# One of two input row buffers begins 48 bytes later in its rows, and the split weights that meet it move with it

## The reference

```python
def hybrid_layer(x, ...):
    h = rms_norm(x, norm1_w)
    (rq, rk, rv, rg, dq, dk, dv, cb, cc, cx, gates) = [h @ w_in[:, s:e] for s, e in column_bounds()]
    ...
    merged = (g[:, :, 0] * (ret @ w_branch[0]) + g[:, :, 1] * (diff @ w_branch[1])
              + g[:, :, 2] * (conv @ w_branch[2]))
    x = x + merged @ w_out
    u = jnp.square(jax.nn.relu(rms_norm(x, norm2_w) @ w_up))
    return x + u @ w_down

def second_block(x, ...):
    proj = hn_p @ w_in[l]
    ...
    mix = (gate_sb * (sb @ w_sb_out[l]) + gate_gla * (o @ w_gla_out[l])) @ w_o[l]
    h = h + _rmsnorm(mix, norm_mix_post[l])
    up = hn @ w_ffn_up[l]
    act = jax.nn.gelu(_causal_dwconv(up, conv_w[l], conv_b[l]), approximate=True)
    ffn = (act * (hn @ w_ffn_gate[l])) @ w_ffn_down[l]
```

## Time and profile before

| | us |
|---|---|
| median of 3 runs (2092.0 to 2096.83) | 2092.36 |
| the profiled execution | 2091.41 |
| its span, first to last instruction | 2089.6 |
| TensorE busy in it | 2076.5 |
| VectorE busy | 1240.4 |
| ScalarE busy | 830.3 |
| GpSimd busy | 164.5 |

### The profile page before, as it was taken

One profiled execution on the slowest core, in us unless ns is written; L12 is line 12 of the kernel. 1 busy time (PEld: TensorE's weight loads), 2 busy tenths in 40 slices (PEclk: granted clock), 3 DMA queues, 4 the chain that ended last, 5 costly groups with the idle time before them and its releaser, 6 DMA issues.

```text
span 2089.6 us, 33866 instructions
## 1 busy us (share of the span) xinstructions
PE 2076.5 (99%) x13662; PEld 1840.2 (88%) x13662; DVE 1240.4 (59%) x1847; ACT 830.3 (40%) x1305; POOL 164.5 (8%) x146
## 2 busy tenths in 40 slices
PE   9999999999999999999999999999999999999998
PEld 8998988898888788898898888999999998889897
DVE  7775434565555555767664666367855567546364
ACT  4333222433444444434434467344434344222233
POOL 0012000030000000132120000022300000000000
PEclk9999999999999999999999999999999999999999
DMA  4343221522222233332322321331133322332323
GB/s 152 111 175 107 86 77 61 203 80 83 72 70 72 88 115 97 111 109 79 115 90 92 91 93 41 94 129 52 62 105 131 99 81 87 96 100 91 101 91 101
DMA packets 55356, 203.27 MB, mean 97 GB/s; under 512 B 6960, under 2 KB 7344, under 8 KB 54336
## 3 DMA queue, kind: packets, MB, share of 16 engines
q1 hardware_dynamic: 49248, 177.56, 26.3%
q10 hardware_dynamic: 5024, 20.70, 2.6%
q0 software_dynamic: 960, 3.24, 0.5%
HBM read 190.91 MB, written 10.57 MB: 96 GB/s over the span
## 4 chain that ended last, share of the span: by engine, by line
PE 93%; DVE 4%; ACT 2%; issue 0%; DMA 0%; POOL 0%; DVEq 0%; SPq 0%; ACTq 0%
PE ps L2234 68%; PE ps L2358 7%; PE ps L2834 5%; PE ps L2700 1%; PE ps L2482 1%; PE ps L2507 1%; PE ps L2435 1%; PE ps L2765 1%; PE ps L2606 1%; DVE kk_r L1884 1%; PE ps L2521 1%; ACT kk L1018 1%; ACT kk L1019 1%; PE ps L2587 0%; PE ps L2743 0%; PE ps L2414 0%
## 5 line engine op out<-in xcount | busy, mean ns | idle before, releaser
L603 ACT ACTIVATE wh<-wraw 128x1024 fp32r<-128x1024 f32 x284 | 300.1, 1057 | 730.7 <-PE ps L2234 611.6
L1288 DVE TENSOR_TENSOR wl<-wraw,wh 128x1024 fp32r<-128x1024 f32 x298 | 365.9, 1229 | 129.7 <-ACT wh L603 125.8
L2234 PE MATMUL ps<-xh,wh 128*128 128x256 f32 (+3 forms) x1800 | 322.6, 324 | 0.9 <-DVE tmp L1321 0.6
L2234 PE MATMUL ps<-xl,wh 128*128 128x256 f32 (+3 forms) x1800 | 315.5, 320 | 0.0
L2234 PE MATMUL ps<-xh,wl 128*128 128x256 f32 (+3 forms) x1800 | 315.4, 320 | 0.0
L2234 PEld LDWEIGHTS ps<-xh,wh 128*128 128x128 f32 x1800 | 262.7, 188 | 29.9 <-issue 2.4
L2234 PEld LDWEIGHTS ps<-xl,wh 128*128 128x128 f32 x1800 | 263.8, 188 | 25.4
L2234 PEld LDWEIGHTS ps<-xh,wl 128*128 128x128 f32 x1800 | 263.8, 188 | 25.2
L2234 PE MATMUL ps<-bh,wh 128*128 128x512 f32 (+3 forms) x1296 | 230.3, 321 | 0.3 <-ACT wh L603 0.2
L2234 PE MATMUL ps<-bl,wh 128*128 128x512 f32 (+3 forms) x1296 | 226.7, 319 | 0.0
L2234 PE MATMUL ps<-bh,wl 128*128 128x512 f32 (+3 forms) x1296 | 226.7, 319 | 0.0
(11 more groups left out here) (533 smaller groups left out, 2770.9 us busy)
## 6 DMA issues: line engine op xcount, KB each, us to landing
wraw<-weights_dram SPq DMA_DIRECT2D x299, 512.0 KB, 3.6
qq<-weights_dram SPq DMA_DIRECT2D x12, 512.0 KB, 4.1
kk<-weights_dram SPq DMA_DIRECT2D x12, 512.0 KB, 4.5
hf<-tables_dram POOLq DMA_DIRECT2D x12, 264.0 KB, 3.0
res<-x_t_dram SPq DMA_DIRECT2D x4, 528.0 KB, 7.1
res<-x_t_dram ACTq DMA_DIRECT2D x1, 2112.0 KB, 8.8
res_dram<-res ACTq DMA_DIRECT2D x1, 2112.0 KB, 6.4
res<-res_dram ACTq DMA_DIRECT2D x1, 2112.0 KB, 15.7
```

The source lines that it names most:

```text
L603: nc.scalar.activation(strip_at(wh, n, slot), wraw[:, slot], ACT.Copy).then_inc(hi_done, 1)
L1288: nc.vector.tensor_tensor(strip_at(wl, n, slot), wraw[:, slot], strip_at(wh, n, slot).bitcast(F32), ALU.subtract)\
L2234: last = nc.tensor.matmul(o, strip_at(w, number, slot)[:, c, :], a[:, c, tok], start=(k == 0), stop=(k == len(steps) - 1))
```

## The change

The b rows begin at column 12 of their 576 (ROW_B), the x rows at column 0 (ROW_X). A table `ROWS` says for each strip which buffer it reads, and `PLACE` adds 12 elements (48 bytes) for strips that read b. The first down strip of a glu group is given the place of the group's first up strip, 12, which is also that of the other down strips now. In the last up group of the first FFN the loops of ScalarE and VectorE are written out, because the strip split ahead in their last turn belongs to x.

```diff
-ROW = 576
+ROW, ROW_X, ROW_B = 576, 0, 12
@@
-PLACE = [T - USED if w == USED else 0 for w in WIDTH]
+
+
+ROWS = [ROW_X] * NSTRIP
+for _name in ("sb_main", "gla_lr", "gla_main", "gla_gates", "w_o"):
+    ROWS[START[_name]:START[_name] + dict(PHASES)[_name]] = [ROW_B] * dict(PHASES)[_name]
+for _n in range(8):
+    ROWS[START["conv_out"] + 4 * (_n // 2) + 2 + _n % 2] = ROW_B
+    ROWS[START["diff_out"] + 8 + _n] = ROW_B
+for _n in (1, 3) + tuple(4 * k + 2 + j for k in range(1, 4) for j in range(2)):
+    ROWS[START["ret_out"] + _n] = ROW_B
+for _g in range(4):
+    ROWS[START[f"ffn{_g}up"]:START[f"ffn{_g}down"]] = [ROW_B] * 8
+for _g, _n in enumerate(FFN2_GROUPS):
+    ROWS[START[f"glu{_g}down"]:START[f"glu{_g}down"] + _n] = [ROW_B] * _n
+PLACE = [r + (T - USED if w == USED else 0) for r, w in zip(ROWS, WIDTH)]
 for _g in range(len(FFN2_GROUPS)):
-    PLACE[START[f"glu{_g}down"]] = T - USED
+    PLACE[START[f"glu{_g}down"]] = PLACE[START[f"glu{_g}up"]]
@@
-def first_then_loop(eng, count, body):
-
-    body(0)
-    with eng.Fori(1, count) as i:
-        body(i)
@@
-        (xh, xl), (bh, bl) = ([r[:, :, 0:T] for r in two_of] for two_of in (x_rows, b_rows))
+        (xh, xl), (bh, bl) = ([r[:, :, first:first + T] for r in two_of]
+                              for two_of, first in ((x_rows, ROW_X), (b_rows, ROW_B)))
@@
-                    first_then_loop(act, KC // 2, up_strips)
+                    for i in range(KC // 2):
+                        up_strips(i)
@@
-                    first_then_loop(dve, KC // 2, up_strips)
+                    for i in range(KC // 2):
+                        up_strips(i)
```

## The result

| | before | after |
|---|---|---|
| median, us | 2092.14 (2091.72 to 2096.83, 5 runs) | 2101.18 (2101.16 to 2101.51, 5 runs) |
| profiled execution / its span, us | 2091.41 / 2089.6 | 2101.16 / 2099.3 |
| TensorE busy, us | 2076.5 | 2085.4 |

The ratio is 1.0039 with a 95% interval of 1.0025 to 1.0054 (it goes by the means, which the one run before at 2096.83 pulls; the medians give 1.0043). So the kernel became slower, by about 0.4%, and the interval lies wholly above 1. The time lies in the range given (2086 to 2105), but not where the forecast's own case was (2088 to 2096).

What follows compares the result with a forecast made beforehand. The prediction took TensorE, through the pace of back-to-back matmuls, to bound the kernel. Its terms, 0 + 0 + 0 - 0.5 - 0.46 + 0.9 + 0 = -0.1 us, gave 2092.3 us, range 2086 to 2105.

Steps and rivals of the forecast that it cites:

- the forecast's own case: Whole kernel: operand differences are kept, so no change, 2092.3 us; chance 0.74.
- step 7: ScalarE and VectorE work on b and weights, two loops written out: same work, slack ahead, cost 0.
- rival C: A table entry mismatching the buffer read puts that strip 48 bytes out, 0.15 us a strip; slower, chance 0.02.
- The condition on the buffers: Buffers lie in declared order, with xh, xl, bh and bl starting at multiples of 256 bytes.
- Step 1: 512-column b strips and down product: rows/weights bytes past a multiple of 256 go 64/64 to 112/112; 0, at most +6.4 ns each.
- step 5: First down strips, 24 matmuls in each of 3 groups, lose their 48-byte difference: 6.4 ns each, -0.46 us.
- Rival A: Place itself matters: 512-column streams beginning 48 bytes past a 64-byte line stall, 1800 x 6.4 ns, +11.5 us, 2103.9; chance 0.14.
- Step 2: Interleaved T strips with b (256 + 272 columns), 184 x 3 pairs, move from 0/64 to 48/112: 0.
- Step 3: Interleaved USED strips with b (256 + 260 columns), 240 x 3 pairs, 48/112 to 96/160: 0, bounds 6.4 ns either way.
- Rival B: New places remove the extra stall of paired strips, 768 USED and 552 T pairs: faster, 2082.5 us; chance 0.10.
- Step 4: Six T strips done by halves: 256-column matmuls fall from 117.5 to 113.8 ns, -0.5 us; 272-column ones unchanged.
- Step 6: New boundaries where x and b placements meet, weights loading while old rows stream: +0.9 us, bounds 0 and 1.9.

Runs made afterwards that it cites:

- both_64: Changed kernel with b rows and the weights that meet them both 64 bytes later instead of 48 (ROW_B = 16); 2091.98 us.
- both_32: Changed kernel with b rows and their weights both 32 bytes later instead of 48 (ROW_B = 8); 2093.03 us, then 2092.73 over 10 runs, ratio 1.0003.
- both_16: Changed kernel with b rows and their weights both 16 bytes later instead of 48 (ROW_B = 4); 2101.93 us.
- w_plus_64: Changed kernel with b rows back at their old place (ROW_B = 0) and all split weights 64 bytes further in their slots; 2124.38 us.
- rows_only: Changed kernel with b rows 48 bytes later but the weights left at their old places; 2107.09 us.

## Why the prediction was wrong, and where it was right

**The frame held.** TensorE's back-to-back pace was the only way in which the change could act; step 7 (engines, loops) and rival C cost nothing that can be seen, as both_64 and both_32 show, which contain the same table and loops. The condition on the buffers held for their order, and the base of 128 bytes changes no difference.

**Step 1 failed**, and with it the forecast: its 1872 matmuls of 512 columns, taken at 0, came to +5.2 us (SEQ strips with b) and +1.75 (down product, with step 5's -0.16 in it). Each runs at 231.0 ns on average at 112/112 instead of 226.8. What failed is the transfer: "where a pair begins made no difference as long as both operands move together" was read from 256-column pairs at two places and carried to 512-column streams at a third place. both_16 and after against both_32 and both_64 show that the place does count there, with the difference kept. The assumption behind it that only differences modulo 64 count, which made 0/64 and 64/64 the same difference, was wrong too (w_plus_64).

**Rival A** had the sign and its test (1.86 to 1.87 us a pass; measured 1.84 to 1.87). Its price failed: it took the 6.4 ns of the first down strip for the price of the place 112, where it is that of the difference 112/64 (rows_only: 233.3). The place by itself costs 3.3 to 6.6, 4.2 on average. It also left out the pairs. 1800 x 6.4 = 11.5 against 1872 at 3.7 = 7, and 2.8 from the pairs: two errors that nearly cancel (2103.9 against 2101.2). Its boundary, a 64-byte line, was wrong as well.

**Step 2 failed for a second reason.** T pairs were given "today's place of USED strips", at 0, but rose by 3.4 ns (240.0 to 243.4). The place was the same, 48/112, but the second piece has 272 columns and not 260. The reading that the 12 columns more are their share (5.0 ns; 12 x 0.443 is 5.3) was a coincidence: at 48/112 the same 12 columns cost 243.4 - 235.0 = 8.4 ns.

**Step 3**: +1.7 ns a pair (+1.2 us), inside its bounds of 6.4 either way. Rival B had no support anywhere: no placement tried made pairs faster on average. Its price also counted 768 USED pairs where 240 x 3 = 720 are interleaved; the other 48 are matmuls by halves.

**Step 4 was right**: 117 to 113 ns, -0.6 us forecast as -0.5, the 272 unchanged. Here row and edit were the same shape at the same place.

**Step 5 was right in kind, wrong in size**: the first down strips fell from 233.3 to 231.2, 72 x 2.2 = -0.16 us and not -0.46, because what they fell to is the pace of 112/112 and not 226.7.

**Step 6**: x SEQ strips +0.2 and the rest +0.3, so at most 0.5 us, inside its 0 to 1.9 and below the 0.9 taken; whether the rest is all of this kind wasn't shown.

**The rule on read ports** (the Trainium skill, TensorE: Matmul & The Clock Gate, Step-by-step: what each phase is for) by which loading weights takes nothing from the running matmul would have given 2092.4 for the change and for every kernel here that leaves no column out. The runs disagree: moving only the weights, by 64 bytes, changes the pace from 226.8 to 233.3 and costs 32 us. How the two operands come to hinder each other isn't shown.

**What stays open.** Why 32 bytes is the boundary for matched streams of 512 columns and hardly matters at 496; whether start, end or length of the stream carries it; and what about its entry sends one up group to 230.0 and the next to 233.3. It is also open why the sign of a difference counts at 16 and 64 bytes and not at 48. No experiment separated the entry from the place.

## What to carry to other kernels

Where matmuls follow each other without a gap, the bytes at which the moving rows and the stationary weights begin are a tuning parameter: the change cost 0.4% of this kernel's time, and w_plus_64 1.5%. For streams of 512 columns the best found is both at the same offset modulo 256, on a multiple of 32 bytes; for pairs of shorter ones it was 64 bytes apart. Measure it in your own kernel, and treat any layout change of either buffer as a change to the time of every product that reads it. Carry a pace from one row to another only if shape and both places are the same: step 4 did so and was right; step 1 changed shape and place, step 2 the shape. And read paces group by group before averaging, since a mean can stand for a mixture of two paces.

## What the runs showed of the hardware that was not expected

- **A few steady paces instead of a continuum.** All kernels ran at a granted clock of 1.0 or 0.999 of 2.4 GHz, so a period is 0.417 ns. The paces of 512 columns are then 544 periods (226.7 ns), 552 (230.0), 554.7 (231.1), 556 (231.7) and 560 (233.3), and 549 (228.9) with the operands 64 bytes apart; those of 500 are 536 and 544; those of 496 are 528, 533.3, 536 and 544. Three of those for 512 are multiples of 8. The fastest is the columns plus 32 for 512 and 496, but plus 36 for 500: unshifted, 12 columns fewer saved 8 periods or none, and 16 fewer saved 16 at best. A product's time is then not its columns by a constant (0.443 ns in my step 1): 500 columns cost 0.447 or 0.453.
- **At 64/64, 96/96 and 128/128 a group that starts slow recovers** to 226.7 within two strips; at 80/80 and 112/112 none does in 192 matmuls.
- **The sign of a mismatch counts at 16 and 64 bytes and not at 48**: 112/64 and 64/112 are both 233.3, but a moving operand 64 bytes further on runs at 228.9 in most groups and one 64 bytes short at 233.3 in all, whether it is the rows or the weights that move.
- **Identical strips in identical kernels can run at different paces** in different groups of one execution (230.0 and 233.3), and yet the totals of five executions agree within 0.35 us. The traces of both_32 and of its timed executions show the 56 SEQ strips with b at the same 56 paces, within 0.1 ns, so what picks the pace repeats from execution to execution.
